# Head norms by a held block of ones: sums with channels on partitions, root and reciprocal over 640 columns

## The chip, the cores and the metric

The kernel runs on one core of a Trainium2 chip. The metric is the device time of one execution in microseconds (us); a lower number is better. The core has five engines with queues of their own that meet only at semaphores: TensorE (PE, with its weight loads as PEld), VectorE (DVE), ScalarE (ACT), GpSimd (POOL) and SyncE (SP, which issues most transfers).

## The reference, cut to what matters

One inference step of a two-layer backbone for 128 context tokens and 512 latent tokens, 640 tokens in all, with 1,024 channels. Each layer runs four token mixers side by side. Two of them end in a norm over each head's 64 channels:

```python
def head_layernorm(x):                      # retention, after which * silu(g)
    mu = jnp.mean(x, axis=-1, keepdims=True)
    var = jnp.mean(jnp.square(x - mu), axis=-1, keepdims=True)
    return (x - mu) * lax.rsqrt(var + NORM_EPS)

def rmsnorm(x, gain):                       # differential attention
    y = x * lax.rsqrt(jnp.mean(x * x, axis=-1, keepdims=True) + NORM_EPS)
    return y * gain
```

Both have 4 heads of 64 channels, so 256 channels for 640 tokens. The mean in retention is already gone from the values when the norm begins, so that both norms need the sum of 64 squares, a root, a reciprocal and a product.

## The kernel before, in words

Mixer outputs lie with channels on partitions: a tile `o_t[0]` of 128 partitions by 2 halves (`c2`) by 640 tokens, two heads to a half. Their squares lie beside them in `ret_sq` (retention) and `o_sq` (differential attention). What a norm needs is one number for each head and token, spread over that head's 64 partitions.

The kernel before makes it in a detour. `head_sums` (line 1045) loads each 128x128 piece of the squares as the held operand of a matmul and moves the two columns `side` through it, ten matmuls for a norm; the sums come out with tokens on partitions, 20 columns. ACT takes the root over those 20 columns, DVE the reciprocal, and `widen` (lines 2512, 2514) writes each of the 20 out 64 times. `turn_rstd` (line 1051) turns the result in ten transposes, so that channels are on partitions again.

The order of each engine's work is written out by hand, and each engine takes its own list strictly in order. What stands around the two norms:

- Retention. PE runs `in_product(2, ret_norm)`, the third block of the input projection, line 1027, tile by tile. `ret_norm(0)` sits at its middle, `ret_norm(1)` behind its first finished tile and `ret_norm(2)` behind the second. PE goes on with gate chunk 8 (line 896), then waits for `rope_done` and transposes the rotated queries and keys (line 1297). ACT takes the root (`ret_root`, line 1769), rounds the next weight unit (`round_unit`, line 1634), copies the five finished tiles (`take_z`) and rounds another unit. POOL turns a rounded unit into its low part (line 855), and the raw buffer is free when that is done. DVE works through the norm, then the rotation `rope` of four tiles (lines 2301, 2305, 2307), then the parting of the normed output into high and low halves.
- Differential attention. Its norm stands in the preparation of the fourth mixer (MLA). PE numbers its products there with `slot()`: product `k` may start once ACT has taken product `k - 4` out of its bank. Products 0 to 3 are two query turns, a latent turn and a key turn (four copies of 32 partitions on ACT, line 1975); then come `head_sums`, five query products (`uq`, line 1386), the two `turn_rstd`, the key and value products (`ukv`, lines 1399 and 1404), and the turns of the rotated queries (line 1411), which wait for `rope_done`. DVE's order there is: four weight copies (line 2573), `widen`, `rope` over four tiles of `z_mq`, the two products of the norm (line 2582), low weights (line 2586), the parting of the output, and the softmax of `attention(3)`.

Of the kernel before, what the change touches and what calls it, by code (L numbers as in the profile page):

```python
# [25 lines left out]
ALU = mybir.AluOpType  # L26
# [291 lines left out]
def build(nc, a, outs):  # L318
# [3 lines left out]
    with ctx:  # L322
# [21 lines left out]
        ones = at("ones", [P, P])  # L344
# [46 lines left out]
        ret_rec = at("ret_rec", [P, 2 * T, 2, 64], offset=OR)  # L391
        o_rec = at("o_rec", [P, 2 * T, 2, 64], offset=Z0 + 5120)
# [79 lines left out]
        def bank(b, lo=0, hi=BANK):  # L472
            return ps[:, b * BANK + lo:b * BANK + hi]
# [70 lines left out]
        rv_mm, rv_act, rx_done, rx_mm = Signal("ret_square_sums"), Signal("ret_rms"), Signal("ret_rstd_widened"), Signal("ret_rstd_turned", 2)  # L544
        rx_read, ox_done = Signal("ret_rstd_used", 2), Signal("diff_rstd_widened")
# [8 lines left out]
        MLA_ITEMS = 4 + 1 + T + 2 + 2 + (T + 1) + 4  # L554
# [78 lines left out]
        def mla_bank(k):  # L633

            return (0, 2, 4, 6)[k % 4]
# [90 lines left out]
        def raw_released(u):  # L726

            kind, i, split, li = UNITS[u]
            if split:
                return low_ready(li, SPLIT_KEYS.index((kind, i)))  # L730
            if kind == "mod":
                return [(mod_mm, counts(li)(mod_mm, MOD_ORDER.index(i) + 1))]
            return [(mla_mm, counts(li)(mla_mm, {"uq": 5 + T, "ukv": 7 + T + 2 + T + 1}[kind]))]
# [126 lines left out]
        def _(pe):  # L860
# [11 lines left out]
            pe.wait_ge(made.sem, 4)  # L872

            for li in range(DEPTH):
# [165 lines left out]
                def head_sums(sq_, b):  # L1040

                    for c2 in range(2):
                        for t in range(T):
                            c0 = 2 * (T * c2 + t)
                            last = mm(bank(b, c0, c0 + 2), sq_[:, c2, t * P:(t + 1) * P], c("side"), start=True, stop=True)
                    return last

                def turn_rstd(rec, c2, b):

                    for t in range(T):  # L1050
                        last = tr(bank(b, t * P, t * P + P), rec[:, T * c2 + t].rearrange("p j d -> p (j d)"), ident)
                    return last

                def ret_norm(part):

                    if part == 0:
                        pe.wait_ge(ro_done.sem, now(ro_done, T))
                        pe.wait_ge(rg_done.sem, now(rg_done, T))
                        head_sums(ret_sq, 5).then_inc(rv_mm.sem, 1)
                    else:  # L1060
                        pe.wait_ge(rx_done.sem, now(rx_done, 1))
                        if part == 2:
                            pe.wait_ge(rx_read.sem, now(rx_read, 1))
                        turn_rstd(ret_rec, part - 1, 5).then_inc(rx_mm.sem, 1)
# [223 lines left out]
                for r in range(3):  # L1288
                    if r == 0:
                        pe.wait_ge(rx_read.sem, now(rx_read, 2))  # L1290
# [87 lines left out]
                head_sums(o_sq, slot()).then_inc(mla_mm.sem, 1)  # L1378
# [10 lines left out]
                pe.wait_ge(ox_done.sem, now(ox_done, 1))  # L1389
                for c2 in range(2):  # L1390
                    turn_rstd(o_rec, c2, slot()).then_inc(mla_mm.sem, 1)
# [212 lines left out]
        def _(sc):  # L1604
# [4 lines left out]
            sc.wait_ge(made.sem, 4)  # L1609
# [6 lines left out]
            for li in range(DEPTH):  # L1616
# [149 lines left out]
                def ret_root():  # L1766

                    sc.wait_ge(rv_mm.sem, now(rv_mm, 1))
                    act_(st5[:, 2, :], bank(5, 0, 4 * T), ACT.Sqrt, bias=eps_c[:], scale=1.0 / 64).then_inc(rv_act.sem, 1)
# [129 lines left out]
                ret_root()  # L1899
# [78 lines left out]
                sc.wait_ge(mla_mm.sem, now(mla_mm, k + 1))  # L1978
                act_(st5[:, 2, :], bank(mla_bank(k), 0, 4 * T), ACT.Sqrt, bias=eps_c[:], scale=1.0 / 64).then_inc(mla_done.sem, 1)
                k += 1  # L1980
# [4 lines left out]
                for c2 in range(2):  # L1985
                    take(o_rms[:, c2, :], P, TOK)
# [116 lines left out]
        def _(ve):  # L2103
            V = nc.vector
            tt, ts, stt = V.tensor_tensor, V.tensor_scalar, V.scalar_tensor_tensor
            V.memset(ones[:], 1.0).then_inc(made.sem, 1)
# [3 lines left out]
            ve.wait_ge(made.sem, 4)  # L2110
# [24 lines left out]
            for li in range(DEPTH):  # L2135
# [383 lines left out]
                ve.wait_ge(rv_act.sem, now(rv_act, 1))  # L2519
                widen(ret_rec).then_inc(rx_done.sem, 1)  # L2520
                for c2 in range(2):
                    ve.wait_ge(rx_mm.sem, now(rx_mm, c2 + 1))
                    tt(ret_g[:, c2, :], ret_g[:, c2, :], bank(5, 0, TOK), ALU.mult).then_inc(rx_read.sem, 1)
                    ve.wait_ge(rx_read.sem, now(rx_read, c2 + 1))
                    stt(o_t[0][:, c2, :], o_t[0][:, c2, :], 0.5, ret_g[:, c2, :], ALU.mult, ALU.mult).then_inc(ret_o.sem, 1)
# [51 lines left out]
                rope(z_mq[:, 1:T, 256:384].rearrange("p t (h c) -> p t h c", h=4), 4, 8, c("c8"), c("s8"), rope_tmp[3][:],  # L2577
                     lambda t: ve.wait_ge(mla_done.sem, now(mla_done, 5 + t + 1)))\
# [167 lines left out]
```

## Time and profile before

| | |
|---|---|
| median of 3 runs | 2323.56 us (2323.31 to 2325.69) |
| profiled execution, first to last instruction | 2320.6 us |
| the rest, median run against that span | 2.96 us |
| PE busy | 2286.9 us, 99% |
| DVE, ACT, POOL busy | 1272.8, 926.8, 747.8 us |
| mean granted TensorE clock | 0.996 |

The profiled execution has a span, which begins with its first instruction and ends with its last. Its own device time is not given apart from the span; the third row of the table sets the span against the median run. An engine that is busy all the time sets the end; what the others do matters where that engine waits for them. Times of the chain of waits lie some 0.15 us behind those of the timeline for the same PE work, since the chain counts from where the matmuls' modelled ends free the engine.

### The profile page before, as it was taken

The page shows a single profiled execution, that of the slowest core. Times are in us where ns is not written, and L with a number is a line of the kernel's source. Part 1 is how long each engine was busy: PE and PEld are TensorE (multiplying, and loading weights), DVE is VectorE, ACT ScalarE, POOL GpSimd, SP SyncE. Part 2 cuts the span into 40 slices and gives each one's busy share as a digit, 9 for nine tenths or more (in the row PEclk, how much of TensorE's full clock was granted, in tenths as well). Part 3 has the DMA queues.
Part 4 walks back from the last instruction along what each step waited for, and adds up shares of the span by engine and source line. Part 5 has one row for each costly group of instructions (what it writes and reads, how often), then busy time and mean ns, then how long its engine had stood idle before and what let it go on. Part 6 is the DMA issues. An engine that isn't in the chain of part 4 may idle for free.

```text
span 2320.6 us, 40593 instructions
## 1 busy us (share of the span) xinstructions
PE 2286.9 (99%) x17116; PEld 2061.5 (89%) x17116; DVE 1272.8 (55%) x2230; ACT 926.8 (40%) x1767; POOL 747.8 (32%) x498
## 2 busy tenths in 40 slices
PE   7999999999999999999999999999999999999998
PEld 6888898888989998998988879888889899899897
DVE  4446458644336763763663473685444467547556
ACT  3335346633335331331363352555442443223223
POOL 0331321111333544543422303121123435544442
PEclk9999999999999999999999999999999999999999
DMA  9313222223232324223242142222232332222211
GB/s 326 130 57 122 75 95 81 78 75 122 96 115 73 91 91 128 73 91 123 78 143 69 39 134 91 86 67 92 74 110 84 108 91 74 75 71 77 87 60 68
DMA packets 221907, 221.62 MB, mean 96 GB/s; under 512 B 10583, under 2 KB 191391, under 8 KB 221471
## 3 DMA queue, kind: packets, MB, share of 16 engines
q1 hardware_dynamic: 212999, 193.77, 26.2%
q10 hardware_dynamic: 8727, 25.27, 3.2%
q8 instruction: 136, 2.23, 0.4%
q14 instruction: 45, 0.36, 0.0%
HBM read 209.90 MB, written 9.11 MB: 94 GB/s over the span
## 4 chain that ended last, share of the span: by engine, by line
PE 92%; DVE 3%; ACT 3%; issue 1%; POOL 1%; DMA 0%; SPq 0%; POOLq 0%; DVEq 0%; ACTq 0%
PE ps L896 50%; PE ps L1027 12%; PE ps L1562 11%; PE ps L1484 4%; PE ps L1168 3%; PE ps L1185 2%; PE ps L916 1%; PE ps L1129 1%; PE ps L1144 1%; PE ps L992 1%; PE ps L1114 1%; PE ps L1150 1%; PE ps L1386 1%; PE ps L907 1%; POOL w_lo L855 1%
## 5 line engine op out<-in xcount | busy, mean ns | idle before, releaser
L855 POOL TENSOR_TENSOR w_lo<-raw,w_hi 128x512 fp32r<-128x512 f32 (+1 forms) x486 | 737.6, 1548 | 1550.7 <-ACT w_hi L1634 996.8
L896 PE MATMUL ps<-h_hi,w_hi 128*128 128x320 f32 (+2 forms) x2368 | 615.2, 312 | 0.0
L896 PE MATMUL ps<-h_lo,w_hi 128*128 128x320 f32 (+2 forms) x2368 | 607.0, 309 | 0.0
L896 PE MATMUL ps<-h_hi,w_lo 128*128 128x320 f32 (+2 forms) x2368 | 606.7, 309 | 0.0
L896 PEld LDWEIGHTS ps<-h_hi,w_hi 128*128 128x128 f32 x2368 | 412.8, 188 | 7.1 <-issue 4.6
L896 PEld LDWEIGHTS ps<-h_lo,w_hi 128*128 128x128 f32 x2368 | 413.4, 188 | 0.2
L896 PEld LDWEIGHTS ps<-h_hi,w_lo 128*128 128x128 f32 x2368 | 413.3, 188 | 0.0
L1634 ACT ACTIVATE w_hi<-raw 128x2048 fp32r<-128x2048 f32 (+2 forms) x110 | 203.8, 1852 | 268.5 <-PE ps L1562 94.6
L1562 PE MATMUL ps<-w_hi,a_hi 128*128 128x512 f32 x440 | 172.3, 392 | 0.6 <-POOL w_lo L855 0.6
L2646 DVE TENSOR_SCALAR conv<-u_pad,vcol 128x642 f32<-128x642 f32 x88 | 90.1, 1024 | 150.9 <-ACT u_pad L2071 149.3
L1562 PE MATMUL ps<-w_lo,a_hi 128*128 128x512 f32 x440 | 171.3, 389 | 0.0
L1562 PE MATMUL ps<-w_hi,a_lo 128*128 128x512 f32 x440 | 171.2, 389 | 0.0
L1027 PE MATMUL ps<-w_hi,h_hi 128*128 128x512 f32 (+1 forms) x440 | 163.0, 371 | 0.8 <-DVE h_lo L2199 0.8
L1027 PE MATMUL ps<-w_hi,h_lo 128*128 128x512 f32 (+1 forms) x440 | 161.4, 367 | 0.0
L1027 PE MATMUL ps<-w_lo,h_hi 128*128 128x512 f32 (+1 forms) x440 | 161.0, 366 | 0.0
L2344 DVE TENSOR_REDUCE stat<-ps 128x1 f32<-128x640 f32 (+3 forms) x160 | 107.7, 673 | 84.5 <-PE ps L1150 53.4
L2079 ACT ACTIVATE usig<-conv 128x642 f32<-128x642 f32 x44 | 32.7, 744 | 257.7 <-DVE conv L2650 257.7
L2071 ACT ACTIVATE u_pad<-ps,vcol 128x128 f32<-128x128 f32 (+3 forms) x264 | 91.8, 448 | 89.8 <-PE ps L896 89.8
L2650 DVE SCALAR_TENSOR_TENSOR conv<-u_pad,vcol,conv 128x642 f32<-128x642 f32 x88 | 116.8, 1327 | 3.1
L2648 DVE SCALAR_TENSOR_TENSOR conv<-u_pad,vcol,conv 128x642 f32<-128x642 f32 x88 | 116.5, 1324 | 3.1
L1813 ACT ACTIVATE probs<-ps,stat 128x640 f32<-128x640 f32 (+3 forms) x136 | 90.4, 666 | 69.2 <-DVE stat L2351 68.5
L1562 PEld LDWEIGHTS ps<-w_hi,a_hi 128*128 128x128 f32 x440 | 82.6, 188 | 18.6 <-POOL w_lo L855 1.4
(347 smaller groups left out, 3474.0 us busy)
## 6 DMA issues: line engine op xcount, KB each, us to landing
raw<-in_w_mod SPq DMA_DIRECT2D x44, 1024.0 KB, 5.1
raw<-in_w_up SPq DMA_DIRECT2D x88, 512.0 KB, 4.8
raw<-in_w_gate SPq DMA_DIRECT2D x32, 1024.0 KB, 5.3
raw<-in_w_in SPq DMA_DIRECT2D x16, 1024.0 KB, 5.2
raw<-in_w_down SPq DMA_DIRECT2D x16, 1024.0 KB, 5.1
w_br<-in_w_branch ACTq DMA_DIRECT2D x8, 1024.0 KB, 4.9
raw<-in_w_out SPq DMA_DIRECT2D x8, 1024.0 KB, 5.0
raw<-in_w_down SPq DMA_DIRECT2D x8, 768.0 KB, 4.4
```

What stands on the lines that cost most here:

```text
L855: ins = nc.gpsimd.tensor_tensor(w_lo[part_slot(li, s)][:, c0:c1], raw[HOME[u]][:, c0:c1], w_hi[part_slot(li, s)][:, c0:c1].bitcast(F32), A ...
L896: ins = mm(out, w_at(w_hl[wi]), at_(x_hl[xi]), start=first and q == 0, stop=final and q == 2)
L1027: last = mm(bank(b, 0, n), (h_hi, h_lo)[xi][:, k, t * P:(t + 1) * P], w_hl[wi][:, k4, :], start=k == 0 and q == 0, stop=k == KD - 1 and q ...
L1484: last = mm(bank(b), (mix_hi, mix_lo)[xi][:, k, row_cols(t)], w_hl[wi][:, k4, :], start=k == 0 and q == 0, stop=k == KD - 1 and q == 2)
L1562: last = mm(bank(b), (a_hi, a_lo)[xi][:, sl, at_], w_hl[wi][:, k4, :], start=k == 0 and q == 0, stop=k == nj - 1 and q == 2)
L1634: act_(w_hi[part_slot(li, s)][:, 0:n], raw[HOME[u]][:, 0:n], ACT.Copy).then_inc(hi_done.sem, 1)
L1813: act_(prob(m)[:, 0:nk], bank(score_bank(m), c0, c0 + nk), ACT.Exp, bias=bias, scale=SCALES[br], accum_out=stat[:, 2, m % 8:m % 8 + 1]).th ...
L2071: ins = act_(u[:, d0:d0 + n], bank(b, c0, c0 + n), ACT.Identity, bias=bias)
L2344: V.tensor_reduce(stat[:, 0, col], bank(b, c0, c0 + nk), AX.X, ALU.max).then_inc(vstep.sem, 1)
L2646: ts(cv, u[:, 0:PADDED], col(WCONV[0]), col(BCONV), ALU.mult, ALU.add).then_inc(vstep.sem, 1)
L2648: stt(cv, u[:, 1:1 + PADDED], col(WCONV[1]), cv, ALU.mult, ALU.add).then_inc(vstep.sem, 1)
L2650: ins = stt(cv, u[:, 2:2 + PADDED], col(WCONV[2]), cv, ALU.mult, ALU.add)
```

## The change

A matrix `blocks` takes the place of an unused matrix of ones: 128x128, with ones in the two 64x64 blocks on the diagonal and zeros beside them. It is the held operand, and the squares move through it, 512 and then 128 columns for each half. Each of the 128 output partitions then holds the sum of its own head's 64 squares, so neither widening nor turning is left. ACT takes the root over 640 columns, once for each half, and DVE the reciprocal over 640 columns. In retention the second half's sums stand behind the first finished tile, and wait for the first root, since both use the same bank. In the fourth mixer's preparation the sums are two numbered products, and the two norm products move ahead of the rotation.

```diff
-        ones = at("ones", [P, P])
+        blocks = at("blocks", [P, P])
-        MLA_ITEMS = 4 + 1 + T + 2 + 2 + (T + 1) + 4
+        MLA_ITEMS = 4 + 2 + T + 2 + (T + 1) + 4
 # PE
-                def head_sums(sq_, b):
-                    for c2 in range(2):
-                        for t in range(T):
-                            c0 = 2 * (T * c2 + t)
-                            last = mm(bank(b, c0, c0 + 2), sq_[:, c2, t * P:(t + 1) * P], c("side"), start=True, stop=True)
-                    return last
-                def turn_rstd(rec, c2, b):
-                    for t in range(T):
-                        last = tr(bank(b, t * P, t * P + P), rec[:, T * c2 + t].rearrange("p j d -> p (j d)"), ident)
+                def head_sums(sq_, c2, b):
+                    for c0, c1 in ((0, BANK), (BANK, TOK)):
+                        last = mm(bank(b, c0, c1), blocks[:], sq_[:, c2, c0:c1], start=True, stop=True)
                     return last
                 def ret_norm(part):
                     if part == 0:
                         pe.wait_ge(ro_done.sem, now(ro_done, T))
                         pe.wait_ge(rg_done.sem, now(rg_done, T))
-                        head_sums(ret_sq, 5).then_inc(rv_mm.sem, 1)
+                    elif part == 1:
+                        pe.wait_ge(rv_act.sem, now(rv_act, 1))
                     else:
-                        pe.wait_ge(rx_done.sem, now(rx_done, 1))
-                        if part == 2:
-                            pe.wait_ge(rx_read.sem, now(rx_read, 1))
-                        turn_rstd(ret_rec, part - 1, 5).then_inc(rx_mm.sem, 1)
+                        return
+                    head_sums(ret_sq, part, 5).then_inc(rv_mm.sem, 1)
 # PE, fourth mixer
-                head_sums(o_sq, slot()).then_inc(mla_mm.sem, 1)
+                for c2 in range(2):
+                    head_sums(o_sq, c2, slot()).then_inc(mla_mm.sem, 1)
...
-                pe.wait_ge(ox_done.sem, now(ox_done, 1))
-                for c2 in range(2):
-                    turn_rstd(o_rec, c2, slot()).then_inc(mla_mm.sem, 1)
 # ACT
-                def ret_root():
-                    sc.wait_ge(rv_mm.sem, now(rv_mm, 1))
-                    act_(st5[:, 2, :], bank(5, 0, 4 * T), ACT.Sqrt, bias=eps_c[:], scale=1.0 / 64).then_inc(rv_act.sem, 1)
+                def ret_root(c2):
+                    sc.wait_ge(rv_mm.sem, now(rv_mm, c2 + 1))
+                    act_(ret_sq[:, c2, :], bank(5, 0, TOK), ACT.Sqrt, bias=eps_c[:], scale=1.0 / 64).then_inc(rv_act.sem, 1)
...
-                ret_root()
+                ret_root(0)
+                ret_root(1)
                 round_unit()
                 take_z(2)
 # ACT, fourth mixer
-                sc.wait_ge(mla_mm.sem, now(mla_mm, k + 1))
-                act_(st5[:, 2, :], bank(mla_bank(k), 0, 4 * T), ACT.Sqrt, bias=eps_c[:], scale=1.0 / 64).then_inc(mla_done.sem, 1)
-                k += 1
+                for c2 in range(2):
+                    sc.wait_ge(mla_mm.sem, now(mla_mm, k + 1))
+                    act_(o_rms[:, c2, :], bank(mla_bank(k), 0, TOK), ACT.Sqrt, bias=eps_c[:], scale=1.0 / 64).then_inc(mla_done.sem, 1)
+                    k += 1
                 for t in range(T):
                     take(z_mq[:, t, :], P, 384)
                 for q in range(2, 4):
                     round_quarter(q)
-                for c2 in range(2):
-                    take(o_rms[:, c2, :], P, TOK)
 # DVE
-            V.memset(ones[:], 1.0).then_inc(made.sem, 1)
+            for lo in range(0, P, 64):
+                for col in range(0, P, 64):
+                    V.memset(blocks[lo:lo + 64, col:col + 64], float(lo == col)).then_inc(made.sem, 1)
...
-                def widen(rec):
-                    V.reciprocal(st5[:, 3, :], st5[:, 2, :]).then_inc(vstep.sem, 1)
-                    ve.wait_ge(vstep.sem, step())
-                    return V.tensor_copy(rec[:].rearrange("p a j d -> p (a j) d"), st5[:, 3, :].unsqueeze(2).to_broadcast([P, 4 * T, 64]))
-                widen(ret_rec).then_inc(rx_done.sem, 1)
                 for c2 in range(2):
-                    ve.wait_ge(rx_mm.sem, now(rx_mm, c2 + 1))
-                    tt(ret_g[:, c2, :], ret_g[:, c2, :], bank(5, 0, TOK), ALU.mult).then_inc(rx_read.sem, 1)
+                    ve.wait_ge(rv_act.sem, now(rv_act, c2 + 1))
+                    V.reciprocal(ret_sq[:, c2, :], ret_sq[:, c2, :]).then_inc(vstep.sem, 1)
+                    ve.wait_ge(vstep.sem, step())
+                    tt(ret_g[:, c2, :], ret_g[:, c2, :], ret_sq[:, c2, :], ALU.mult).then_inc(vstep.sem, 1)
                     stt(o_t[0][:, c2, :], o_t[0][:, c2, :], 0.5, ret_g[:, c2, :], ALU.mult, ALU.mult).then_inc(ret_o.sem, 1)
 # DVE, fourth mixer
-                ve.wait_ge(mla_done.sem, now(mla_done, 5))
-                widen(o_rec).then_inc(ox_done.sem, 1)
+                for c2 in range(2):
+                    ve.wait_ge(mla_done.sem, now(mla_done, 4 + c2 + 1))
+                    V.reciprocal(o_rms[:, c2, :], o_rms[:, c2, :]).then_inc(vstep.sem, 1)
+                    ve.wait_ge(vstep.sem, step())
+                    stt(o_t[0][:, c2, :], o_t[0][:, c2, :], vcol[:, GDIFF:GDIFF + 1], o_rms[:, c2, :], ALU.mult, ALU.mult).then_inc(diff_o.sem, 1)
                 rope(z_mq[:, 1:T, 256:384] ...).then_inc(rope_done.sem, 1)
-                for c2 in range(2):
-                    ve.wait_ge(mla_done.sem, now(mla_done, 5 + T + c2 + 1))
-                    stt(o_t[0][:, c2, :], o_t[0][:, c2, :], vcol[:, GDIFF:GDIFF + 1], o_rms[:, c2, :], ALU.mult, ALU.mult).then_inc(diff_o.sem, 1)
```

## Rows read from the trace of the kernel before

**Rows 1.** The page: busy engines, and the chain that ended last by engine.
```profile
PE 2286.9 (99%) x17116; PEld 2061.5 (89%) x17116; DVE 1272.8 (55%) x2230; ACT 926.8 (40%) x1767; POOL 747.8 (32%) x498
...
PE 92%; DVE 3%; ACT 3%; issue 1%; POOL 1%; DMA 0%; SPq 0%; POOLq 0%; DVEq 0%; ACTq 0%
```

**Rows 2.** Chain of waits at the retention norm, layer 0: start us, us, what.
```profile
151.67 2.13 PE ps L1045 x20
153.80 2.89 PE ps L1027 x12
156.69 0.55 PE ps L1051 x5
...
168.76 3.52 PE ps L896 x24
172.28 1.75 PE ps L1297 x16
```

**Rows 3.** Chain of waits at the retention norm, layer 1.
```profile
1299.81 4.45 PE ps L1027 x12
```

**Rows 4.** Window behind that norm: us, busy of PE, PEld, DVE, ACT, POOL, granted clock, DMA.
```profile
1299.90:1303.40 3.50, 3.50 (x10) 2.68 (x10) 1.10 (x2) 2.03 (x2) 1.40 (x2) 0.52 0.00 0
```

**Rows 5.** Chain of waits at the fourth mixer's preparation, layer 0.
```profile
436.10 2.16 PE ps L1045 x20
438.26 6.66 PE ps L1386 x40
...
451.52 1.09 PE ps L1411 x10
```

**Rows 6.** Timeline of PE at the same place in layer 1: start us, us.
```profile
1585.68 8.46 PE L1386 MATMUL ps<-raw,cq_t 128*128 128x256 f32 x40
```

**Rows 7.** Groups of DVE instructions by shape: count, busy us and mean ns, idle before.
```profile
L2365 DVE RECIPROCAL stat<-stat 128x1 f32<-128x1 f32 x80 | 12.9, 162 | 12.9 <-ACT probs L1813 11.5
...
L2525 DVE SCALAR_TENSOR_TENSOR o_t<-o_t,ret_g 128x640 f32<-128x640 f32 x4 | 3.6, 896 | 0.1
...
L2567 DVE TENSOR_TENSOR z<-z,st 128x640 f32<-128x640 f32 x2 | 1.6, 825 | 0.1
...
L2512 DVE RECIPROCAL st<-st 128x20 f32<-128x20 f32 x4 | 1.1, 278 | 20.1 <-ACT st L1769 18.0 <-ACT st L1979 2.1
...
L2415 DVE RECIPROCAL dec_t<-dec_t 128x12 f32<-128x12 f32 x2 | 0.5, 228 | 0.1
```

**Rows 8.** Groups of ACT instructions by shape, a copy of 640 columns from PSUM.
```profile
L1967 ACT ACTIVATE cq_t<-ps 128x640 f32<-128x640 f32 x4 | 2.6, 716 | 0.0
```

**Rows 9.** Timeline of DVE and POOL behind the retention norm, layer 0.
```profile
162.22 0.75 DVE L2301 TENSOR_TENSOR rope<-z,const 128x96 f32<-128x96 f32 x4
...
164.07 0.76 DVE L2301 TENSOR_TENSOR rope<-z,const 128x96 f32<-128x96 f32 x4
...
170.82 0.56 DVE L2307 TENSOR_TENSOR z<-z,rope 128x384 f32<-128x384 f32 x1
...
156.00 5.62 POOL L855 TENSOR_TENSOR w_lo<-raw,w_hi 128x512 fp32r<-128x512 f32 x4 [8.46 <-ACT w_hi L1634]
```

**Rows 10.** Timeline of ACT in the fourth mixer's preparation, layer 0.
```profile
436.96 3.23 ACT L1975 ACTIVATE kr_t<-ps 32x768 f32<-32x768 f32 x4
440.21 1.28 ACT L1979 ACT_TABLE_LOAD   x1
```

**Rows 11.** Timeline of DVE and POOL in the same stretch.
```profile
442.87 0.49 DVE L2301 TENSOR_TENSOR rope<-z_mq,const 128x32 f32<-128x32 f32 x4
...
443.93 0.49 DVE L2301 TENSOR_TENSOR rope<-z_mq,const 128x32 f32<-128x32 f32 x4
...
448.02 1.24 DVE L2307 TENSOR_TENSOR z_mq<-z_mq,rope 128x128 f32<-128x128 f32 x1
449.18 3.72 DVE L2582 SCALAR_TENSOR_TENSOR o_t<-o_t,vcol,o_rms 128x640 f32<-128x640 f32 x2
...
446.56 5.66 POOL L855 TENSOR_TENSOR w_lo<-raw,w_hi 128x512 fp32r<-128x512 f32 x4 [33.89 <-ACT w_hi L1646]
```

More of the change, by code:

```diff
@@ L390, in build @@
         ret_sq = at("ret_sq", [P, 2, TOK], offset=OR)
-        ret_rec = at("ret_rec", [P, 2 * T, 2, 64], offset=OR)
-        o_rec = at("o_rec", [P, 2 * T, 2, 64], offset=Z0 + 5120)
         ret_g = at("ret_g", [P, 2, TOK], offset=PTR)
@@ L543, in build @@
         rg_mm, rg_act, rg_done = Signal("ret_gate_turned", T), Signal("ret_gate_tanh", T), Signal("ret_gate_ready", T)
-        rv_mm, rv_act, rx_done, rx_mm = Signal("ret_square_sums"), Signal("ret_rms"), Signal("ret_rstd_widened"), Signal("ret_rstd_turned", 2)
-        rx_read, ox_done = Signal("ret_rstd_used", 2), Signal("diff_rstd_widened")
+        rv_mm, rv_act = Signal("ret_square_sums", 2), Signal("ret_rms", 2)
         ret_o, diff_o = Signal("ret_normed", 2), Signal("diff_normed", 2)
@@ L732, in raw_released @@
                 return [(mod_mm, counts(li)(mod_mm, MOD_ORDER.index(i) + 1))]
-            return [(mla_mm, counts(li)(mla_mm, {"uq": 5 + T, "ukv": 7 + T + 2 + T + 1}[kind]))]
+            return [(mla_mm, counts(li)(mla_mm, {"uq": 6 + T, "ukv": 6 + T + 2 + T + 1}[kind]))]
         def parts_released(s):
@@ L871, in _ @@
             pe.wait_ge(cond_done.sem, 2)
-            pe.wait_ge(made.sem, 4)
+            pe.wait_ge(made.sem, 7)
             for li in range(DEPTH):
@@ L1289, in _ @@
                     if r == 0:
-                        pe.wait_ge(rx_read.sem, now(rx_read, 2))
+                        pe.wait_ge(rv_act.sem, now(rv_act, 2))
                     b = (4, 0, 2)[r]
@@ L1608, in _ @@
             act_(stat[:, 0:2, :].rearrange("p a b -> p (a b)"), cond[:], ACT.Sigmoid).then_inc(cond_sig.sem, 1)
-            sc.wait_ge(made.sem, 4)
+            sc.wait_ge(made.sem, 7)
             act_(stat[:, 6, 0:1], eps_c[:], ACT.Sqrt)
@@ L2109, in _ @@
             V.memset(cond_c[:], 0.0).then_inc(made.sem, 1)
-            ve.wait_ge(made.sem, 4)
+            ve.wait_ge(made.sem, 7)
             ve.wait_ge(cond_t.sem, 1)
@@ L2518, in _ @@
                 tt(flat(w3_lo[:]), flat(w_br[:]), flat(w0_hi[:]).bitcast(F32), ALU.subtract).then_inc(w0_done.sem, 1)
-                ve.wait_ge(rv_act.sem, now(rv_act, 1))
-                widen(ret_rec).then_inc(rx_done.sem, 1)
                 for c2 in range(2):
-                    ve.wait_ge(rx_mm.sem, now(rx_mm, c2 + 1))
-                    tt(ret_g[:, c2, :], ret_g[:, c2, :], bank(5, 0, TOK), ALU.mult).then_inc(rx_read.sem, 1)
-                    ve.wait_ge(rx_read.sem, now(rx_read, c2 + 1))
+                    ve.wait_ge(rv_act.sem, now(rv_act, c2 + 1))
[3 more added lines that the diff above has]
+                    ve.wait_ge(vstep.sem, step())
                     stt(o_t[0][:, c2, :], o_t[0][:, c2, :], 0.5, ret_g[:, c2, :], ALU.mult, ALU.mult).then_inc(ret_o.sem, 1)
@@ L2574, in _ @@
                 ins.then_inc(w2_high.sem, 1)
-                ve.wait_ge(mla_done.sem, now(mla_done, 5))
-                widen(o_rec).then_inc(ox_done.sem, 1)
+                for c2 in range(2):
+                    ve.wait_ge(mla_done.sem, now(mla_done, 4 + c2 + 1))
+                    V.reciprocal(o_rms[:, c2, :], o_rms[:, c2, :]).then_inc(vstep.sem, 1)
+                    ve.wait_ge(vstep.sem, step())
+                    stt(o_t[0][:, c2, :], o_t[0][:, c2, :], vcol[:, GDIFF:GDIFF + 1], o_rms[:, c2, :], ALU.mult, ALU.mult).then_inc(diff_o.sem, 1)
                 rope(z_mq[:, 1:T, 256:384].rearrange("p t (h c) -> p t h c", h=4), 4, 8, c("c8"), c("s8"), rope_tmp[3][:],
-                     lambda t: ve.wait_ge(mla_done.sem, now(mla_done, 5 + t + 1)))\
+                     lambda t: ve.wait_ge(mla_done.sem, now(mla_done, 6 + t + 1)))\
                     .then_inc(rope_done.sem, 1)
-                for c2 in range(2):
-                    ve.wait_ge(mla_done.sem, now(mla_done, 5 + T + c2 + 1))
-                    stt(o_t[0][:, c2, :], o_t[0][:, c2, :], vcol[:, GDIFF:GDIFF + 1], o_rms[:, c2, :], ALU.mult, ALU.mult).then_inc(diff_o.sem, 1)
                 ve.wait_ge(w2_high.sem, now(w2_high, 1))
```

## The prediction

> **What bounds the kernel now.** I read the page first. PE is busy 99% of the span, and 92% of the chain that ended last is PE [rows 1]; so time is won only by taking work off PE, and lost wherever PE is made to wait. I then read the chain of waits around the two places where a norm stands, in both layers. There, too, the chain is PE alone: sums, projection, transposes, projection, without a gap [rows 2, 5]. The reader is to see in those rows that the norms' other halves, on ACT and DVE, hide behind PE, and by how much. In retention DVE ends the rotation at 170.82 + 0.56 = 171.4 [rows 9] and PE asks for it at 172.28 [rows 2]: 0.9 us of cover. In the fourth mixer DVE ends its rotation at 448.02 + 1.24 = 449.3 [rows 11], and PE asks at 451.52 [rows 5]: 2.2 us of cover. Last I looked at what DVE's instructions cost by shape, since the change puts a new one on it.
>
> **PE's own work.** Removed in each norm: the 20 narrow matmul instructions, 2.13 us, and ten transposes, 2 x 0.55 us in retention [rows 2], the same in the fourth mixer (2.16 us of sums [rows 5], ten transposes at the same price); 3.2 us for a norm. Added: four plain f32 matmuls, of 512 and 128 columns for each half. The nearest row of that kind is the query product: 40 instructions, half of 256 and half of 128 columns, for the 20 matmuls that the code writes, so each f32 matmul runs twice. That is 7,680 columns in 6.66 us [rows 5], 0.867 ns a column. A half costs 2 x 640 x 0.867 = 1.11 us and a norm 2.2 us. PE gains 1.0 us for each norm, 4.0 us in all, if nothing makes it wait.
>
> **The clock.** Behind the narrow matmuls in layer 1, the next twelve projection matmuls took 4.45 us [rows 3] where layer 0's took 2.89 [rows 2]; the granted clock was 0.52 there [rows 4], the lower level of 1.2 GHz, though PE was never idle. In the fourth mixer the query product behind the same matmuls took 8.46 us in layer 1 [rows 6] against 6.66. Layer 0 shows neither. Two dips cost 1.56 and 1.7 us. With the squares moving instead of two columns, PE streams through those stretches, and I count both dips as gone: 3.3 us won.
>
> **ACT.** A root over 640 columns from PSUM is bounded by the copy of the same shape, 0.72 us, or 0.65 where two follow each other [rows 8]. In retention the second root waits for PE's second sums, behind the first tile, and the rounding of the next weights is queued behind it. Sums: 151.67 + 1.11 = 152.8, 2.9 us of projection to 155.7, second sums to 156.8. Now POOL starts 2.2 us behind the end of the sums (153.80 to 156.00), with the narrow root and the rounding between them; with the wide root it is some 2.6 us, so POOL starts its 5.6 us [rows 9] at 159.4 and ends at 165.0, and the transfer that its raw buffer frees leaves 3.4 us later. Gate chunk 8 needs these weights at 168.76 - 1.0 = 167.8: hidden with 2.8 us to spare. The five tile copies catch up by the third tile. I cost this at nothing; without the cover it would be up to 3.5 us a layer, though most of that falls into the wait below.
>
> **The reciprocal on DVE.** This decides. No row has a reciprocal over 640 columns. The rows have 162 ns for one column, 228 for 12, 278 for 20 [rows 7]: 6.0 ns for each further column, then 6.25 ns, near enough a straight line. Products of 640 columns take 825 and 896 ns [rows 7], 1.3 to 1.4 ns a column with all overhead. By the line 640 columns take 0.16 + 639 x 0.006 = 4.0 us, by its last stretch 0.28 + 620 x 0.00625 = 4.15 us. The lower bound is that of any 640-column operation, 0.8 us. I take 4.15, from the two rows that are nearest in width. Four norms bring eight of them, 33 us of DVE time, where `widen` and its reciprocal over 20 columns cost 1.1 us a norm.
>
> The Trainium skill, page "VectorE: DVE Perf Modes", section "First, the fixed hardware budget", says that the reciprocal is an iterative divide with a repeat count of 8, and its specifications give DVE 0.96 GHz. Read as eight cycles a column, that would be an estimate of 5.3 us for 640 columns, where the rows of this case give 4.1. By the page the sum would come out 9.6 us higher (below); the row decides.
>
> **Retention, DVE against PE (layer 0).** First root ready at 152.8 + 0.7 = 153.5. Reciprocal to 157.7, product 0.83 to 158.5, product 0.90 to 159.45; reciprocal to 163.65, two products to 165.4. Behind them in DVE's queue stands the rotation: 1.85 us a tile (164.07 - 162.22 [rows 9]), four tiles to 172.8. It no longer waits for ACT's tiles. PE, 1.0 us ahead, would ask for it at 171.3 and gets it at 172.95, so it waits 1.65 us and is 0.7 us later than now. In layer 1 the dip's 1.56 us is also gone: 0.9 us earlier. Retention together: -0.2 us.
>
> **Fourth mixer, DVE against PE (layer 0).** First PE's numbered products. The key turn's copies leave ACT at 440.19 and the table load follows to 441.49 [rows 10]; the first root is out at 442.2, the second at 442.85. Sums now take PE from 436.1 to 438.3. With one product more ahead, the query products move one place in the numbering: the second waits for the key copies (440.2), the third for the first root (442.2). They end at 442.2 + 3 x 1.33 = 446.2, the following products take 5.5 us (now from 438.26 + 6.66 + 1.1 for the transposes = 446.0 to 451.52 [rows 5]), and PE asks for the rotation at 451.7. So the won transposes are already used up by those waits.
>
> DVE: reciprocal from 442.25 to 446.4, product 0.9 to 447.3, reciprocal to 451.5, product 1.86 (half of 3.72, since POOL works beside it [rows 11]) to 453.4. Only then does the rotation begin, which now begins at 442.87, beside the query products: four tiles at 1.06 us (443.93 - 442.87) and 0.4 us of POOL's disturbance to 458.0. PE starts its turns at 458.1 instead of 451.5, so 6.6 us later, after 6.4 us of standing idle. What is late next: the key and query copies, DVE's low weights and the softmax of the third attention, all of which shift with PE. DVE's low weights and the parting already stand between the rotation and the softmax, and with the norm's products (3.72 us now) moved ahead of the rotation less stands behind it than before, so nothing further is held back. In layer 1 the dip of 1.7 us is gone: 4.9 us later.
>
> **The clock after the wait.** No row shows PE idle for 6 us in mid-kernel. Bounds: nothing, or two dips of the size seen. I take one dip of 1.7 us for each wait, 3.4 us, nearest to what [rows 3, 4] show after mere thin work. The Trainium skill, page "TensorE: Matmul & The Clock Gate", section "What's actually happening", says the same in general: the throttled clock is the default and activity releases it. By that rule the dip comes for certain here, and the sum stays as it is.
>
> **Start.** Three small memsets more on DVE, ahead of its wait for PE's first transpose, which itself waits for a transfer: nothing; without that cover three times a short instruction of 0.16 us.
>
> **Sum.** Retention -0.2, fourth mixer 6.6 + 4.9 = 11.5, clock 3.4: +14.7 us. Against the profiled span: 2320.6 + 14.7 = 2335.3. The median of the runs lies 2.96 us above that span, so 2323.56 + 14.7 = 2338.3 us.
>
> **Rivals.**
> - *The reciprocal is cheap* (ends on the other side). If it ran over 640 columns like other operations, 0.8 us, DVE would be through the fourth mixer's rotation by 451 and PE would never wait for it. Then PE gains 1.0 us in retention and loses 0.2 to the numbering in the fourth mixer, and both dips go: 2 x (-1.0) + 2 x 0.2 - 3.3 = -4.9, 2318.7 us. For it: only that no wide row exists. Against it: three widths on one line. It decides below about 1.0 us for a reciprocal; break-even of the whole lies near 2 us, half of the line. Chance 0.08.
> - *Something in between*, 2 to 3.3 us a reciprocal, or the rotation's wait partly covered: 2324 to 2332 us. Chance 0.08.
> - *Eight cycles a column*: 5.3 us, 1.2 us more for each of eight, all of it on PE's wait: +9.6, 2347.9 us. That is the page's rule above as a mechanism of this kernel; [rows 7] speak against it. Chance 0.07.
> - *The clock is harsher*: two dips a wait and the old dips stay: +3.4 + 3.3, 2345 us. Chance 0.09. *No dip after the waits*: 2334.9, which I count within the forecast.
> - The forecast: chance 0.68, its own range 2333 to 2343.
>
> **How the numbers follow.** 0.2% is 4.6 us, about what a measurement of this kernel can tell from no change. The range takes in the forecast, the eight-cycle case, the harsher clock and the upper part of the in-between one, and leaves out the cheap reciprocal: 2329 to 2348. Faster is the rival of a cheap reciprocal, 0.07 of its 0.08 (its price lies just over the bound); same is the lower half of the in-between case and the rest, 0.06; slower everything else, 0.87.
>
> **What the profile after would show.** Reciprocals of 128x640 near 4.1 us each, x8. In the fourth mixer PE idle for some 6 us ahead of the first turns of `z_mq`, released by DVE's rotation; PE idle 1 to 2 us ahead of the transposes behind gate chunk 8. Sums in 1.1 us a half. No granted clock near 0.5 behind the sums, but a dip behind the long wait. The prediction is wrong if a reciprocal takes under 3 us, if the products' numbering doesn't hold PE as worked out, or if PE makes up the wait later, for which I see no slack in a chain that is PE at 92%.

## The result and the profile after

The changed kernel takes 2351.98 us (2351.36 to 2352.13, 4 runs), where the kernel before took 2323.72 on the same chip: a ratio of 1.0119 [1.0107, 1.0131]. The prediction was slower, 2338.3 us, with a range of 2329 to 2348; the sign is right, the size is half of what came, and the time lies outside the range. Its sum was +14.7 us; the spans differ by 2349.5 - 2320.6 = 28.9.

The views below show where the 28.9 us are. First the waits of PE, after: line waited at, engine and line waited for, total, times, longest. In the kernel before neither of the first two rows has a counterpart; PE went through both places without a gap [rows 2, 5].

```profile
PE ps L1285 <- issue: 12.9, 2, 6.5
PE ps L1397 <- DVE z_mq L2295: 11.8, 2, 5.9
...
PE ps L1375 <- ACT kr_t L1962: 1.3, 2, 0.6
PE ps L1375 <- ACT o_rms L1967: 1.1, 2, 0.5
```

L1285 are the transposes behind the retention norm, L1397 the first turns of the fourth mixer. Each stands once in each layer. The second row is the wait that the prediction worked out (6.4 us). The first should have been 1.65 us and is 6.5. The last two are the waits that the numbering of the products brings in the fourth mixer. "issue" in the first row means that the profile names no releaser; in the code PE waits there for `rope_done`, and it starts at 177.75, 0.1 us behind the end of DVE's rotation (below).

The chain of waits at the retention norm, layer 0, after, beside [rows 2]:

```profile
151.91 1.08 PE ps L1040 x4
152.99 2.77 PE ps L1024 x12
155.76 1.08 PE ps L1040 x4
156.84 10.92 PE ps L1024 x48
167.76 3.52 PE ps L893 x24
171.28 6.47 issue
177.75 3.65 PE ps L1285 x16
```

The sums take 1.08 us a half, and gate chunk 8 ends at 171.28; both as predicted (1.11, 171.3). Then PE stands still for 6.47 us, and the same 16 transposes take 3.65 us where they took 1.75. The windows behind say why (columns: us, busy of PE, PEld, DVE, ACT and POOL, granted clock, DMA share, GB/s):

```profile
171.00:178.00 7.00, 0.53 (x4) 0.30 (x4) 6.90 (x9) 1.03 (x2) 5.01 (x4) 0.68 0.00 0
178.00:184.00 6.00, 6.00 (x28) 6.00 (x28) 1.87 (x2) 3.94 (x6) 0.00 (x0) 0.52 0.00 0
184.00:190.00 6.00, 6.00 (x45) 5.64 (x44) 1.83 (x9) 1.85 (x5) 0.00 (x0) 1.00 0.00 0
```

The granted clock is 0.52 in the second window, the level of 1.2 GHz. In finer windows it is 1.00 up to 173.0, 0.50 from 175.0 to 183.5 and 1.00 again from 184.0: it fell while PE stood still, and PE worked for about 6 us at the lower level. What DVE and POOL did while PE waited, in their timelines (start us, us):

```profile
158.90 0.83 DVE L2507 SCALAR_TENSOR_TENSOR o_t<-o_t,ret_g 128x640 f32<-128x640 f32 x1
159.64 4.14 DVE L2503 RECIPROCAL ret_sq<-ret_sq 128x640 f32<-128x640 f32 x1
163.82 1.49 DVE L2505 TENSOR_TENSOR ret_g<-ret_g,ret_sq 128x640 f32<-128x640 f32 x1
...
169.33 0.56 DVE L2295 TENSOR_TENSOR z<-z,rope 128x384 f32<-128x384 f32 x1
169.80 0.76 DVE L2289 TENSOR_TENSOR rope<-z,const 128x96 f32<-128x96 f32 x4
170.59 1.52 DVE L2293 TENSOR_TENSOR z<-z,const 128x384 f32<-128x384 f32 x1
172.15 1.50 DVE L2295 TENSOR_TENSOR z<-z,rope 128x384 f32<-128x384 f32 x1
173.58 2.88 DVE L2289 TENSOR_TENSOR rope<-z,const 128x96 f32<-128x96 f32 x4
176.50 0.56 DVE L2293 TENSOR_TENSOR z<-z,const 128x384 f32<-128x384 f32 x1
...
159.56 5.07 POOL L852 TENSOR_TENSOR w_lo<-raw,w_hi 128x512 fp32r<-128x512 f32 x4 [11.80 <-ACT w_hi L1620]
170.28 5.73 POOL L852 TENSOR_TENSOR w_lo<-raw,w_hi 128x512 fp32r<-128x512 f32 x4 [5.66 <-ACT w_hi L1620]
```

The rotation runs at 1.86 us a tile until 170.3. Then POOL begins its second unit, and for as long as it works the same operations take 1.5 us instead of 0.56, and 2.88 instead of 0.76. The rotation ends at 177.65, where the prediction had 172.8: about 4.1 us are this collision and 0.7 us the product at 163.82, which took 1.49 us for 0.82 beside POOL's first unit. In the kernel before POOL's second unit began at 171.28, 0.1 us ahead of the rotation's end at 171.38 [rows 9]:

```profile
171.28 6.98 POOL L855 TENSOR_TENSOR w_lo<-raw,w_hi 128x512 fp32r<-128x512 f32 x4 [9.66 <-ACT w_hi L1634]
```

In the fourth mixer the wait is the length of what stands ahead of the rotation on DVE. Its timeline in layer 0, and then a line of PE's with the wait in brackets:

```profile
450.77 4.15 DVE L2559 RECIPROCAL o_rms<-o_rms 128x640 f32<-128x640 f32 x1 [1.45 <-ACT o_rms L1967]
454.96 0.89 DVE L2561 SCALAR_TENSOR_TENSOR o_t<-o_t,vcol,o_rms 128x640 f32<-128x640 f32 x1
455.76 4.15 DVE L2559 RECIPROCAL o_rms<-o_rms 128x640 f32<-128x640 f32 x1
459.94 1.10 DVE L2561 SCALAR_TENSOR_TENSOR o_t<-o_t,vcol,o_rms 128x640 f32<-128x640 f32 x1
460.96 1.55 DVE L2289 TENSOR_TENSOR rope<-z_mq,const 128x32 f32<-128x32 f32 x4
...
466.40 2.40 PE L1397 MATMUL ps<-const,z_mq 128*128 128x128 f32 x10 [5.89 <-DVE z_mq L2295]
```

Last the reciprocal, in the groups of DVE instructions (count, busy us and mean ns), beside the narrow ones in [rows 7]:

```profile
L2503 DVE RECIPROCAL ret_sq<-ret_sq 128x640 f32<-128x640 f32 x4 | 16.6, 4150 | 17.0 <-ACT ret_sq L1755 17.0
L2559 DVE RECIPROCAL o_rms<-o_rms 128x640 f32<-128x640 f32 x4 | 16.6, 4150 | 3.0 <-ACT o_rms L1967 3.0
```

4.15 us, the predicted value. The ledger by the trace, from each norm's sums to the first attention scores behind them: retention takes 8.2 us longer in layer 0 and 5.6 in layer 1 (predicted -0.2 together), the fourth mixer 8.55 and 6.3 (predicted 14.9 with its two clock dips), together 28.7 of 28.9. The dips behind the narrow sums of layer 1 [rows 4] are gone, as predicted.

### The profile page after: what moved, and what is told of

The parts are those of the page before. It is cut to its first block, busy times and chain, and to the rows that moved or that the text cites. A ratio compares the mean times of both kernels' runs of the same rounds, so it can differ in the third digit from the quotient of the medians.

```text
span 2349.5 us, 40416 instructions
## 1 busy us (share of the span) xinstructions
PE 2289.2 (97%) x17028; PEld 2059.1 (88%) x17028; DVE 1302.8 (55%) x2233; ACT 929.7 (40%) x1767; POOL 742.4 (32%) x498
## 4 chain that ended last, share of the span: by engine, by line
PE 90%; DVE 4%; ACT 3%; issue 2%; POOL 1%; DMA 0%; SPq 0%; POOLq 0%; DVEq 0%; ACTq 0%
PE ps L893 50%; PE ps L1024 11%; PE ps L1548 11%; PE ps L1470 3%; PE ps L1156 3%; PE ps L1173 2%; PE ps L913 2%; PE ps L1117 1%; PE ps L1132 1%; PE ps L989 1%; PE ps L1102 1%; DVE o_rms L2559 1%; PE ps L1138 1%; PE ps L904 1%; POOL w_lo L852 1%
## 5 line engine op out<-in xcount | busy, mean ns | idle before, releaser
L1548 PE MATMUL ps<-w_lo,a_hi 128*128 128x512 f32 x440 | 171.3, 389 | 0.0
```

The costliest lines, as they stand in the source:

```text
L1548: last = mm(bank(b), (a_hi, a_lo)[xi][:, sl, at_], w_hl[wi][:, k4, :], start=k == 0 and q == 0, stop=k == nj - 1 and q == 2)
```

## The experiments

Theory A is what the trace after suggests: the reciprocals are the cost, directly in the fourth mixer, and in retention by pushing the rotation into POOL's second unit. All kernels start from the changed one unless said otherwise. The kernel before took 2324.56 (first four), 2324.80 (next four) and 2323.21 us (last three) beside them. Each group ran on another chip, so times are compared as ratios; by the intervals a difference between two ratios is known to some 0.002, or 4 us.

### Reciprocals away, and by half

```diff
-V.reciprocal(ret_sq[:, c2, :], ret_sq[:, c2, :])
+ts(ret_sq[:, c2, :], ret_sq[:, c2, :], 1.0, None, ALU.mult)   # the same for o_rms; the end of the line is left out
```

> The changed kernel with each of the eight reciprocals over 640 columns replaced by a product with 1.0 on the same columns, so both norms multiply by the root instead of dividing by it. Theory A (the length of the reciprocal on VectorE is the cause of all that was lost): without it TensorE waits nowhere, the gain in matmuls and the two clock dips of layer 1 show, and the time is 2319 us, some 5 below the kernel before. Rival B (the wider sums, the wider roots or the new numbering of products cost by themselves): the time stays above 2330.

> The changed kernel with each reciprocal over the first 320 of its 640 columns; the other half of the tokens is multiplied by the root. By the line of the narrow reciprocals one takes 2.15 us. Theory A with a collision (retention's rotation runs into GpSimd's next weight unit only if it is late): VectorE is 4 us earlier in each norm, so retention has neither wait nor collision and wins 3.5 us in the two layers, the fourth mixer keeps a wait of some 2.3 us a layer: 2324 us, the time of the kernel before. Rival C (no collision, the loss goes in proportion to VectorE's time): 8 x 2 us less than the changed kernel, 2336 us.

The first kernel leaves out the reciprocal and multiplies by the root; the second keeps it, but over 320 of 640 columns. Measured: with no reciprocal 2328.97 us, ratio 1.0022 [1.0013, 1.0032]; with half 2347.48, ratio 1.0106 [1.0091, 1.0121]. So taking the reciprocals away returns most of the loss, but not the 2319 that theory A gave; PE still waited 2.5 us at each set of transposes and up to 1.6 at each first turn. And a reciprocal of half the length (2.15 us) returns only 0.0013 of the ratio, 3 us (4.5 by the medians), which can't be told from nothing; PE still waits 6.0 us at the transposes and 4.9 to 5.1 at the turns. Both misses have one reason, seen in DVE's timeline with half the reciprocal (POOL's first unit runs there from 159.47 to 165.7):

```profile
157.63 2.15 DVE L2503 RECIPROCAL ret_sq<-ret_sq 128x320 f32<-128x320 f32 x1
159.81 1.63 DVE L2505 TENSOR_TENSOR ret_g<-ret_g,ret_sq 128x640 f32<-128x640 f32 x1
161.48 1.80 DVE L2507 SCALAR_TENSOR_TENSOR o_t<-o_t,ret_g 128x640 f32<-128x640 f32 x1
163.19 2.95 DVE L2289 TENSOR_TENSOR rope<-z,const 128x96 f32<-128x96 f32 x4
166.17 0.56 DVE L2293 TENSOR_TENSOR z<-z,const 128x384 f32<-128x384 f32 x1
```

In the changed kernel the reciprocal lies beside POOL's first unit, and takes 4.14 us there as elsewhere: it is not slowed. Shortened, it clears the place for the two products and the rotation's first step, and these are: 1.63 + 1.80 + 2.95 us where they take 0.83 + 0.83 + 0.76 alone. Of the 4.0 us saved on the two reciprocals nearly all is paid back to POOL; the second unit takes its share as before, and the rotation ends at 177.07 in place of 177.65. The fourth mixer does the same: there the rotation's first step now lies on POOL's unit and takes 4.95 us in layer 0, where it takes 0.49 alone. With no reciprocal at all the rotation's first step took 4.50 us, and its last tile again met the second unit (1.52 and 1.50).

### The second rounding later; the rotation first

```diff
                 take_z(2)
-                round_unit()
...
                 take_gate(9)
+                round_unit()
```

> The changed kernel with one step moved: ScalarE rounds the weight unit behind the five tile copies only behind gate chunk 9, so GpSimd's low part of it starts behind retention's rotation instead of beside it. Theory A with the collision: the two last rotation tiles take 1.9 us each again, TensorE's wait falls from 6.5 to some 2 us and its clock does not dip behind it: 2339 us, or 2343 if the dip stays. Rival D (the rotation was slow for another reason, as the stores of its input or ScalarE's copies beside it, which stay where they are): 2352 us.

Measured: 2342.96 us, ratio 1.0082 [1.0067, 1.0097], the case of the expectation in which the clock still dips. ACT's rounding releases POOL's second unit; behind gate chunk 9 the unit begins at 183.2. The last tile now takes 0.76, 0.56, 0.56, the rotation ends at 173.5, and the wait at the transposes falls from 6.5 us to 2.4. That is the collision alone, reciprocals untouched: 0.0037 of the ratio, 8.6 us. The remaining 2.4 us stand against the predicted 1.65; the difference is the product that met the first unit. In the chain of waits:

```profile
171.19 2.43 issue
173.62 3.50 PE ps L1285 x16
177.12 3.62 PE ps L893 x24
```

The transposes still take 3.50 us for 1.75 (3.35 in layer 1): with the chunk behind them a dip of 1.8 us in each layer, behind a wait of only 2.4.

In the other kernel the fourth mixer's `rope` stands ahead of the norm in DVE's list, and nothing else is changed.

> The changed kernel with one step moved: in the fourth mixer's preparation VectorE turns to the rotation before the two reciprocals and products, as the kernel before does. Theory A: TensorE no longer waits for the rotation, but the third attention waits for the norm, which ends some 4 us before the point where TensorE now starts it: 2344 us. Rival E (the order is what costs, not the length): the loss of the fourth mixer goes altogether, 2337 us.

Measured: 2349.33 us, ratio 1.0110 [1.0093, 1.0126], no gain that can be told from the changed kernel. The wait at the turns is gone, and one of 4.2 us for the normed heads (in the code PE waits there for `diff_o`) stands at the start of the last attention in each layer; its matmuls run at the lower clock, 0.51 from 468 to 472. Neither expected time came (2344, 2337): most of what was taken off one wait came back in the next, since DVE's 10.7 us of norm still lie ahead of something that PE asks for.

### One norm alone

The fourth mixer as in the kernel before, retention with the change.

> The change in the retention norm alone: the fourth mixer keeps its 20 narrow sums, the turned rstd and the short norm on VectorE. Theory R (read from the trace after: the late rotation meets GpSimd's weight unit, TensorE idles 6.5 us and then runs at a lower clock, both layers): retention carries 13.8 of the 28.9 us, so 2323.6 + 13.8 = about 2337, with two waits of 6.5 us ahead of the transposes. Rival P (the sum of the prediction: retention costs nothing, -0.2 us): 2323 to 2324; the loss would then come only when both norms are changed.

Measured: 2335.11 us, ratio 1.0047 [1.0032, 1.0062]. So retention alone loses 11 us, and the prediction's step of -0.2 us for it is refuted on its own. Both its waits are 6.5 us again. The trace gives 12.4 us for the two places here, 13.8 in the changed kernel, where the transposes and the chunk behind them ran longer at the lower clock. The fourth mixer is then the rest, a ratio of 1.0119/1.0047, some 17 us and by the intervals 12 to 21, against 14.9 by the trace and by the prediction.

### No reciprocal, and both rotations clear of POOL

The product with 1.0 stays in place of each reciprocal; on top of it the roundings that release POOL's units are moved.

```diff
                 ret_root(0)
-                ret_root(1)
                 round_unit()
+                ret_root(1)
                 take_z(2)
-                round_unit()                      # behind gate chunk 9, as above
...
-                for q in range(2, 4):
-                    round_quarter(q)              # to behind the value copies
```

> Each reciprocal is replaced by a product with 1.0 (no reciprocal is computed), and ScalarE's roundings that release GpSimd's units are moved off the rotations: the first between the two roots, the second behind gate chunk 9, the quarters of the fourth mixer behind the value copies. Short reciprocals alone gave 2329.0, with waits of 2.5 us at the transposes and 1.6 us at the turns of the queries. Theory A (what is left there is GpSimd's units beside the late rotations): both waits under 1 us, no clock dip behind them, 2319 to 2322. Rival F (wide roots, f32 sums or the two products on VectorE cost it, wherever GpSimd works): 2326 or more.

Measured: 2319.84 us, ratio 0.9979 [0.9970, 0.9989]. No wait is left at the transposes or at the turns; the window with the transposes reads 1.00. With the first run, where POOL's units stood as before, the parts of the loss can be told apart: 1.0022 with the collisions and 0.9979 without, so what POOL's place beside the rotations cost the run without reciprocals is 10 us. The first unit still meets retention's second half of the norm (1.10, 1.79 and 1.80 us for 0.49, 0.83 and 0.83), and PE waits for nothing there. Theory A holds only together with where POOL works; the wide roots, the f32 sums and the two products cost less than the change saves on PE (rival F is refuted). The prediction's rival of a cheap reciprocal, 2318.7 us, was priced without any such move and would have come out near the 2329 of the first run; only with POOL moved is its number met.

### Versions with the full computation

Half the norm, the rotation, half the norm, in both places, with the two roundings of retention moved as above:

> The full reciprocals, correct order kept: on VectorE each norm is split around its rotation (first half, rotation, second half), and the two roundings of retention are moved as in the run with short reciprocals beside it (between the roots, and behind gate chunk 9). Theory S (only what stands ahead of the rotation counts, the second half finds room behind it): retention's wait falls from 6.5 us to under 1.5, the one at the turns of the queries from 5.9 to some 1.5, and some 2.5 us appear at the start of the last attention, which waits for the normed heads: 2331 to 2336. Rival W (VectorE's total work in the stage is the bound, the wait only moves): retention as with the late rounding (2.4 us) and 5 us at the last attention, 2341 or more.

Measured: 2331.76 us, ratio 1.0034 [1.0022, 1.0046]. The time is within what theory S gave, though its waits fell otherwise. Retention has none left. Its second reciprocal runs from 170.35 to 174.49, when nobody waits for it. In the fourth mixer the wait at the turns is 3.7 us in layer 0 and 4.1 in layer 1, in place of some 1.5, because POOL's unit there now lies on the rotation's second tile, in DVE's timeline:

```profile
447.41 2.65 DVE L2289 TENSOR_TENSOR rope<-z_mq,const 128x32 f32<-128x32 f32 x4
450.09 1.25 DVE L2293 TENSOR_TENSOR z_mq<-z_mq,const 128x128 f32<-128x128 f32 x1
451.37 1.23 DVE L2295 TENSOR_TENSOR z_mq<-z_mq,rope 128x128 f32<-128x128 f32 x1
452.52 0.48 DVE L2289 TENSOR_TENSOR rope<-z_mq,const 128x32 f32<-128x32 f32 x4
```

No version with the full reciprocals and the fourth mixer's rounding moved too was run. The next takes the reciprocal off DVE: ACT takes the logarithm where it took the root, and behind the tile copies the exponential.

```diff
-act_(ret_sq[:, c2, :], bank(5, 0, TOK), ACT.Sqrt, bias=eps_c[:], scale=1.0 / 64)
+act_(ret_sq[:, c2, :], bank(5, 0, TOK), ACT.Ln, bias=eps_c[:], scale=1.0 / 64)
...
+act_(ret_sq[:, c2, :], ret_sq[:, c2, :], ACT.Exp, scale=-0.5)
```

> No reciprocal on VectorE: ScalarE takes the logarithm of each bank in place of the root and, behind the tile copies, the exponential of -0.5 times it; VectorE rotates first and applies the norm after. The roundings are placed as in the run with short reciprocals. Two more passes of some 0.75 us a norm on ScalarE. Theory A (the reciprocals' 4.15 us and what they push into GpSimd's units are the whole loss): 2318 to 2324. Rival L (ScalarE, which copies keys, values and queries out of the banks in the fourth mixer, becomes the bound, and table loads are added): a wait of 2 to 4 us a layer for ScalarE in the fourth mixer, 2327 to 2332.

Measured: 2321.39 us, ratio 0.9989 [0.9979, 0.9999]. In retention PE waits for nothing. No table load is added there, it only moves, since the load ahead of the exponential also serves the gate's tanh behind it; in ACT's timeline:

```profile
168.46 1.28 ACT L1892 ACT_TABLE_LOAD   x1
...
169.75 1.37 ACT L1892 ACTIVATE ret_sq<-ret_sq 128x640 f32<-128x640 f32 x2
171.35 0.53 ACT L1779 ACTIVATE acc<-ps,vcol 128x320 f32<-128x320 f32 x1 [0.24 <-PE ps L894]
```

The fourth mixer still loses: from the start of its sums to the first gate chunk 20.96 us for 19.02 before, of which 0.64 and 0.53 are the two waits for ACT that the numbering brings, as the prediction had it, and 0.63 a third for the query copies. Its interval ends at 0.9999, so that this version is hardly told from the kernel before. That points to the last versions: the change in retention alone, once with the norm split around the rotation and reciprocals kept, once with logarithm and exponential; and, as a control, the kernel before with the second rounding moved.

> The change in the retention norm alone, with its full reciprocals, but VectorE does half a norm, the rotation, half a norm, and ScalarE's roundings stand between the roots and behind gate chunk 9; the fourth mixer as before. Theory S (retention has room for two reciprocals of 4.15 us once neither stands between the rotation and GpSimd's unit): no wait at the transposes, both clock dips of 1.2 GHz behind the narrow sums of layer 1 gone, and TensorE gains about 1 us a norm: 2318 to 2321, a ratio under 0.9985. Rival N (the retention part of the change gains nothing at best): 2323 to 2325.

> The change in the retention norm alone, by logarithm and exponential on ScalarE and the rotation first, roundings placed as before in this series; the fourth mixer as in the kernel before. From the trace of the version with both norms so: retention has no wait left, the fourth mixer from the start of its sums to the first gate chunk takes 20.96 us for 19.02 before. Theory: taking the old fourth mixer back gives these 1.9 us a layer, 2321.4 - 3.9 = about 2317.5, ratio 0.997. Rival: the version is at the level of the one with reciprocals and a split norm beside it (2318 to 2321), because retention has room for either.

> The kernel before with ScalarE's second rounding of that stage moved behind gate chunk 9, and nothing of the change: a control for the versions that carry this move. If the move itself were worth something, this would be below 2323 (ratio under 0.999) and the gain of those versions would not be that of the sums. My theory: the old rotation ends before GpSimd's unit begins, so nothing is gained: 2323 to 2325.

| kernel | us | ratio |
|---|---|---|
| split norm in retention alone | 2320.87 | 0.9986 [0.9977, 0.9995] |
| logarithm in retention alone | 2319.07 | 0.9982 [0.9973, 0.9991] |
| kernel before, rounding moved | 2325.26 | 1.0003 [0.9994, 1.0011] |

Both versions beat the kernel before, by 0.14 and 0.18%. That is real by their intervals, and small. They can't be told apart, so the expected 2317.5 for the second wasn't met and its rival stands: retention has room for either. The control gains nothing: the old rotation had ended when POOL began. It also keeps the layer-1 dip behind the narrow sums, which the split version has lost, both in the window of [rows 4]:

```profile
1299.90:1303.40 3.50, 3.50 (x12) 2.78 (x12) 1.10 (x2) 2.08 (x2) 1.13 (x1) 0.62 0.00 0
```

```profile
1299.90:1303.40 3.50, 3.50 (x16) 2.67 (x16) 2.01 (x1) 2.60 (x2) 0.16 (x1) 1.00 0.03 10
```

The first fence is the control, the second the split version; the granted clock is the third number from the end, 0.62 and 1.00.

The dip behind the fourth mixer's narrow sums is another matter. The expectation had it gone in layer 1 of the split version, which keeps those sums; the query product behind them took 8.32 us in both layers there, 6.66 and 8.32 with the logarithm, and 6.66 in both layers of the control and of the change in retention alone. The same instructions dip in one kernel's profiled execution and not in another's, and the 1.7 us between the two versions' spans (2319.5 and 2317.8) are as much as one such dip. Over all the profiles narrow sums of the fourth mixer were followed by a dip in 4 of 10 places and those of retention in 2 of 4; the sums with `blocks` in none of 38.

## Why the prediction was right in sign and half in size

- **The reciprocal on DVE**: right, 4.15 us each, eight of them. The rival of eight cycles a column is refuted by the same rows. (It came from the Trainium skill, page "VectorE: DVE Perf Modes", section "First, the fixed hardware budget"; its repeat count of 8, read as eight cycles a column, gave an estimate of 5.3 us, and the measurement decides.)
- **PE's own work**: 1.08 us a half for 1.11; PE reached the transposes at 171.28 for 171.3.
- **Fourth mixer, DVE against PE**: right. PE's turns came 6.6 us late in layer 0 and 4.9 in layer 1, after 5.9 us of idling; the numbering held PE at the key copies and the first root, as written, and PE asked for the turns 0.7 us later than before where the sum had 0.2. Two terms missed in opposite directions, which is luck: the second product took 1.10 us for the 1.86 allowed, and the rotation's first step 1.55 us for 0.49, where 0.4 us of disturbance was allowed. The dip behind cost 1.95 us in layer 0 and 1.4 in layer 1, for 1.7.
- **The clock after the wait**: right that it dips, wrong in being counted for the fourth mixer only. Retention's wait is as long, and the dip behind it cost 2.8 us in layer 0 and 1.9 in layer 1, by PE's timeline. Even the short wait that the sum had there was not safe without a dip: 2.4 us of waiting in the run with the late rounding cost 1.8 us in each layer. The two old dips, 3.3 us counted as gone, were gone; but the later profiles show them to come and go with narrow sums, so this term is sized by one execution.
- **Retention, DVE against PE**: this step failed, the overlap of the rotation with POOL, put at nothing. "Behind them in DVE's queue stands the rotation: 1.85 us a tile (164.07 - 162.22 [rows 9]), four tiles to 172.8." The step checked POOL's first unit and its weights, and not where POOL's second unit would lie. Before, the rotation ended 0.9 us ahead of PE's request and just as a POOL unit began; here that unit begins 1.0 us earlier, so any later rotation meets it. In place of 1.65 us the wait was 6.47 us twice. The rows already showed two-input products beside POOL at about twice their time (3.72 us for two) [rows 11], and the sum used that for one product in the fourth mixer and for no rotation tile of retention. In numbers: the waits are 2 x 4.8 = 9.6 us more, the dips that were not counted 2.8 + 1.9 = 4.7; together 14.3, against the 28.9 - 14.7 = 14.2 that were missing.
- **The break-even** of 2 us a reciprocal was wrong for the same reason: with half the length, 2.15 us, the kernel was still 1.06% slower, and with none 0.22%.
- **The start** and **ACT's late rounding**: no wait of PE points to either, as predicted.

## What to carry to other kernels

Before a step is moved later on DVE, lay POOL's timeline over its new place, unit by unit, and price every two-input operation there at what it takes beside POOL. A wait of PE can also cost a stretch at the lower clock behind it, in whichever stage it stands; at these two places every one of 3.7 us and more did, and three of the four of 2.4 to 2.5 us. And where a wide result replaces a narrow one, ask which engine has room at that time: here retention's reciprocals went with a loss of 11 us while both stood ahead of the rotation, and with a small gain once one stood behind it and POOL's unit was out of the way.

## What the runs showed of the hardware

- DVE operations with two SBUF inputs beside POOL's subtractions (5.07 us for four, 1.27 each): 0.56 us becomes 1.50 to 1.52, and four of 128x96 take 2.88 to 4.50 for 0.76. The reciprocal, with one input, took 4.14 us beside the same instructions. POOL's unit is held up too: 5.07 us beside the reciprocal, 6.21 beside the products (with half the reciprocal). The Trainium skill, page "SBUF — State Buffer", section "Who interferes with whom", says that a DVE instruction with two SBUF inputs contends with a GpSimd instruction that reads SBUF, and that one with a single input does not, outside the modes that use both ports; the rotation and the reciprocal agree. I had not weighed it for the rotation. One input alone was no safeguard: beside POOL the product with 1.0 took 1.10 us for 0.49 (both rotations clear), and the cast of the output to its high part 1.89 for 0.82 (no reciprocal).
- The reciprocal's time is a straight line over the whole range measured: 0.16 us for one column, 2.15 for 320, 4.15 for 640, or 6.25 ns a column.
- PE's clock around an idle stretch, in the changed kernel: retention's 6.47 us of idling were followed by some 6 us of work at 0.50 in layer 0 and some 4 us in layer 1. With the late rounding the clock read 1.00 through the 2.4 us of idling and 0.50 from 175 to 177. With no reciprocal 2.5 us of idling were followed by a dip of 1.7 us in layer 0 (transposes 3.47 us) and of 0.2 in layer 1 (1.94). Where retention's wait was gone, its transposes took 1.75 us.
